# Attention in a two-layer block: the squares of q and their high part move from ScalarE to VectorE

## The reference

```
def rms_norm(x, g):
    xf = x.astype(jnp.float32)
    y = xf * lax.rsqrt(jnp.mean(xf * xf, axis=-1, keepdims=True) + EPS)
    return (y * g.astype(jnp.float32)).astype(x.dtype)

def swa_sink_mixer(h, w_in, q_gain, sinks, w_out, k_band, v_band, bias, mask):
    q, z = jnp.split(h @ w_in, 2, axis=-1)
    q = rms_norm(q.reshape(B, T, B_Q_HEADS, B_HD), q_gain) * (B_HD ** -0.5)
    logits = jnp.einsum("bnqkgd,bnskd->bnkgqs", q, k_band).astype(jnp.float32) + bias
    ...
    p = jnp.exp(logits - m)
    probs = p / (jnp.sum(p, axis=-1, keepdims=True) + jnp.exp(sink - m))
    o = jnp.einsum("bnkgqs,bnskd->bnqkgd", probs.astype(v_band.dtype), v_band)
    o = o.reshape(B, T, B_W) * jax.nn.silu(z)
```

## Time and profile before

| | before |
|---|---|
| median of three runs | 1569.17 us |
| lowest and highest run | 1562.31 and 1571.47 us |
| span of the profiled execution | 1562.4 us |
| VectorE busy | 893.4 us (57%) |
| ScalarE busy | 751.1 us (48%) |
| GpSimd busy | 258.1 us (17%) |
| mean granted TensorE clock | 0.999 |

### The profile page before, as it was taken

The page is one execution under the profiler, slowest core; times in us unless marked ns, Lnnn a source line. Parts: engine busy times, 40 slices in busy tenths (PEclk is TensorE's granted clock), DMA queues, the critical chain, the costliest instruction groups (busy, mean ns, idle before and its releaser), DMA issues.

```text
span 1562.4 us, 20671 instructions
## 1 busy us (share of the span) xinstructions
PE 1531.7 (98%) x7650; PEld 1222.0 (78%) x7650; DVE 893.4 (57%) x1681; ACT 751.1 (48%) x1310; POOL 258.1 (17%) x453
## 2 busy tenths in 40 slices
PE   9989999999999999999998999999999999999998
PEld 7878888888878777777776887666678888888877
DVE  5767677776656456666666435554375243443476
ACT  4454455544553346666667314656555241332343
POOL 1033323443313003343343000000000000000000
PEclk9999999999999999999999999999999999999999
DMA  5311111211114332222222231112222223233221
GB/s 202 109 54 54 55 54 55 67 55 55 47 48 153 99 106 73 84 82 68 81 76 68 81 108 63 54 68 68 67 85 91 94 95 108 84 105 95 94 95 54
DMA packets 40163, 127.22 MB, mean 81 GB/s; under 512 B 4576, under 2 KB 9104, under 8 KB 40064
## 3 DMA queue, kind: packets, MB, share of 16 engines
q1 hardware_dynamic: 38112, 121.65, 24.1%
q0 software_dynamic: 1040, 3.27, 0.6%
q10 hardware_dynamic: 912, 0.99, 0.2%
HBM read 122.69 MB, written 2.15 MB: 80 GB/s over the span
## 4 chain that ended last, share of the span: by engine, by line
PE 90%; DVE 5%; ACT 3%; POOL 1%; issue 1%; DMA 0%; SPq 0%; POOLq 0%; ACTq 0%; DVEq 0%
PE ps L833 87%; PE ps L1196 2%; PE ps L976 1%; DVE wl L1945 1%; ACT L L1751 1%; POOL L L2761 1%; DVE h L2595 1%; DVE mo L2589 1%; POOL uc L2731 0%; POOL masks L2729 0%; DVE L L2452 0%; DVE up L2080 0%; DMA wraw<-in_wa 0%; DVE xm L2582 0%; ACT wh L1340 0%
## 5 line engine op out<-in xcount | busy, mean ns | idle before, releaser
L833 PE MATMUL ps<-xr,wh 128*128 128x512 f32 x2752 | 880.1, 401 | 3.5 <-DVE xr L2388 1.2
L833 PEld LDWEIGHTS ps<-xr,wh 128*128 128x128 f32 x2752 | 505.7, 188 | 129.6 <-issue 30.5
L833 PE MATMUL ps<-xr,wl 128*128 128x512 f32 x1376 | 538.4, 391 | 0.0
L1945 DVE TENSOR_TENSOR wl<-wraw,wh 128x1024 fp32r<-128x1024 f32 x214 | 264.5, 1243 | 130.9 <-ACT wh L1340 128.8
L833 PEld LDWEIGHTS ps<-xr,wl 128*128 128x128 f32 x1376 | 258.6, 188 | 56.1
L1340 ACT ACTIVATE wh<-wraw 128x1024 fp32r<-128x1024 f32 x214 | 222.2, 1049 | 85.8 <-PE ps L833 83.8
L833 PE MATMUL ps<-xm,wh 128*128 128x512 f32 x640 | 198.8, 392 | 5.1 <-DVE xm L2582 2.7
L833 PEld LDWEIGHTS ps<-xm,wh 128*128 128x128 f32 x640 | 119.5, 188 | 33.5 <-DVE xm L2582 4.0
L2761 POOL TENSOR_SCALAR L<-L,m 128x256 f32<-128x256 f32 (+1 forms) x128 | 99.2, 794 | 272.2 <-DVE m L2467 272.2
L833 PE MATMUL ps<-xm,wl 128*128 128x512 f32 x320 | 124.7, 390 | 0.0
L1983 DVE SCALAR_TENSOR_TENSOR qkv<-cin,gains,qkv 128x512 f32<-128x512 f32 x96 | 77.3, 807 | 10.6 <-ACT qkv L1370 9.7
(11 more groups left out here) (265 smaller groups left out, 1749.7 us busy)
## 6 DMA issues: line engine op xcount, KB each, us to landing
wraw<-in_wa SPq DMA_DIRECT2D x48, 512.0 KB, 3.7
wraw<-in_wb SPq DMA_DIRECT2D x32, 512.0 KB, 4.0
wraw<-in_wu SPq DMA_DIRECT2D x32, 512.0 KB, 3.6
wraw<-in_wd SPq DMA_DIRECT2D x32, 512.0 KB, 3.7
wraw<-in_wao SPq DMA_DIRECT2D x16, 512.0 KB, 3.7
wraw<-in_wbo SPq DMA_DIRECT2D x16, 512.0 KB, 3.9
wraw<-in_wc SPq DMA_DIRECT2D x16, 512.0 KB, 3.7
bias<-rel_rows SPq DMA_DIRECT2D x16, 256.0 KB, 3.8
```

Source lines behind the costliest of these rows:

```text
L833: return e.matmul(out, w, x, start=start, stop=stop, skip_group_check=True)
L1945: e.tensor_tensor(m.wl[:, i % N_SPLIT, :], m.raw[:, i % N_RAW, :], m.wh[:, i % N_SPLIT, :].bitcast(F), ALU.subtract).then_inc(s.wlo, 1)
```

## The change

ScalarE's part of `qsquares` is gone. VectorE's part now makes all three: the square in float32, the square again with a rounded output, and the remainder. The waits that ScalarE's part had stand ahead of them on VectorE. The signals are the same, now given by VectorE. The part is called at the same place of `follow`.

```
--- ScalarE's program
     @part
-    def qsquares(j):
-        r = m.flat[j % 2]
-        e.wait_ge(s.q, j + 1)
-        if j == 0:
-            e.wait_ge(s.rows, 16)
-        elif j == 1:
-            for g in range(4):
-                e.wait_ge(s.kpad[g], 32)
-        else:
-            e.wait_ge(s.tr_p, 4 * (j - 2) + 4)
-        e.activation(r[:, 512:1024], m.qb[:, j % 3, :], ACT.Square).then_inc(s.hn_sq, 1)
-        e.wait_ge(s.hn_sq, 2 + j + 1)
-        e.activation(m.LR[:, j % 2, 2, :], r[:, 512:1024], ACT.Copy).then_inc(s.hn_hi, 1)
--- VectorE's program
     @part
     def qsquares(j):
-
+        q, sq = m.qb[:, j % 3, :], m.flat[j % 2][:, 512:1024]
+        e.wait_ge(s.q, j + 1)
+        if j == 0:
+            e.wait_ge(s.rows, 16)
+        elif j == 1:
+            for g in range(4):
+                e.wait_ge(s.kpad[g], 32)
+        else:
+            e.wait_ge(s.tr_p, 4 * (j - 2) + 4)
+        e.tensor_tensor(sq, q, q, ALU.mult).then_inc(s.hn_sq, 1)
+        e.tensor_tensor(m.LR[:, j % 2, 2, :], q, q, ALU.mult).then_inc(s.hn_hi, 1)
+        e.wait_ge(s.hn_sq, 2 + j + 1)
         e.wait_ge(s.hn_hi, j + 2)
         e.tensor_tensor(m.LR[:, j % 2, 3, :], m.flat[j % 2][:, 512:1024], m.LR[:, j % 2, 2, :].bitcast(F),
                         ALU.subtract).then_inc(s.hn_lo, 1)
```

More of the change, by code:

```diff
@@ L1720, in qsquares @@
     @part
-    def qsquares(j):
-        r = m.flat[j % 2]
-        e.wait_ge(s.q, j + 1)
-        if j == 0:
-            e.wait_ge(s.rows, 16)
-        elif j == 1:
-            for g in range(4):
-                e.wait_ge(s.kpad[g], 32)
-        else:
-            e.wait_ge(s.tr_p, 4 * (j - 2) + 4)
-        e.activation(r[:, 512:1024], m.qb[:, j % 3, :], ACT.Square).then_inc(s.hn_sq, 1)
-        e.wait_ge(s.hn_sq, 2 + j + 1)
-        e.activation(m.LR[:, j % 2, 2, :], r[:, 512:1024], ACT.Copy).then_inc(s.hn_hi, 1)
-    @part
     def qnorm(j):
```

## The result

The changed kernel takes 1575.63 us (median of six runs, 1575.46 to 1579.41), the kernel before 1568.62 us beside it. The ratio is 1.006 with a 95% interval from 1.0044 to 1.0075: slower by some 7 us by the medians, 9 us by the ratio. The profiled spans are further apart, 1573.7 against 1562.4 us.

What follows compares the result with a forecast made beforehand. TensorE was taken to bound the kernel, busy 1531.7 of 1562.4 us, with VectorE's and ScalarE's latency counting where it waits. 14 x 0.64 = 9.0 plus 0.4 gave +9.4 us on the median 1569.17: 1578.6 us, range 1568 to 1586.

Steps and rivals of the forecast that it cites:

- The unmarked wait: At the head sum TensorE waits for the remainder (line 2429) each pair, too briefly to be marked: 0.23 us a period.
- The order on VectorE: In VectorE's in-order queue the squares stand behind lines 2465 and 2467, so cannot use the 2.67 us idle before.
- The slip: The remainder starts 1.56 instead of 0.92 us after line 2467's start: 0.64 us a pair, 9.0 us for j=1 to 14.
- The 0.05 charged for GpSimd: Delay of VectorE's added work by GpSimd's multiplication of the probabilities (line 2761): 0.05 us a period.
- The 0.10 behind the double wait: The remainder, waiting for both squares, starts 0.10 us late behind its last releaser.
- The last pair: At j=15 0.37 us of cover is left, but TensorE waits for line 2761, held up by the added work: 0.4 us.
- They delay each other: VectorE's instructions and GpSimd's pieces of line 2761 slow one another; 0.05 us a period charged to VectorE.
- No gain from ScalarE's relief: ScalarE loses 20.0 us and rounds a weight tile 1.25 us earlier in a period, costed at no gain.
- Full blocking: Each multiplication and the remainder's start stand behind a whole GpSimd piece: slip 1.31 us, 18 in all, 1588 us; chance 0.13.
- The not-slower case: Squares run in VectorE's idle 2.67 us between lines 2031 and 2465; TensorE's stalls go: 4 us less, 1565 us; chance 0.07.
- The hidden case: The 0.83 us distance is no wait, or multiplications are quick as a copy: 0 to 4 us, 1569 to 1573; chance 0.20.

Runs made afterwards that it cites:

- experiment 1: Changed kernel with VectorE's three instructions issued directly behind q's tile, ahead of line 2465: 1564.94 us, ratio 0.9982 to the kernel before.
- experiment 2: Changed kernel with a third VectorE multiplication, its result overwritten, between the two squares: 1589.6 us, ratio 1.0136 to the kernel before.
- experiment 5: Kernel of experiment 1 with a third multiplication, also placed early, behind line 2031: 1559.97 us in one run.
- experiment 6: Changed kernel with GpSimd's line of probabilities, pairs 0 to 14, held until the next pair's remainder is done: 1576.73 us in one run.
- experiment 7: Changed kernel without the remainder's wait on the first square: 1576.79 us in a single run.
- experiment 8: Changed kernel with the rounded square made as a copy of the first square, not a second multiplication: 1578.74 us in one run.
- experiment 3: Changed kernel with the float32 square back on ScalarE; VectorE makes rounded square and remainder: 1567.81 us, ratio 1.0007 to the kernel before.
- experiment 9: Kernel of experiment 1 again, with more runs beside the kernel before: 1565.59 us, ratio 0.9975.
- the early kernel: The kernel of experiment 1, measured again in experiment 9: 1564.94 and 1565.59 us.

## Why the prediction was right

The way and the size were right: +9.4 us forecast, +7.0 by the medians and 10 at equal clock, and the range holds the measured time. The mechanism is the forecast one. That the size came so close is in part luck (see "What cancels").

- **The unmarked wait.** It was argued from a constant distance of 0.83 us and three spacings in the earlier trace rows. Shown: moved out of the way (experiment 1) it gave 0.23 us a period, the figure priced; with the path longer by 0.56 us (the change) or 1.26 (experiment 2), the period grew by all of it.
- **The order on VectorE.** Shown by the timeline after and by experiments 1 and 5. It is what made the change a loss: in the program's text the squares follow the laying down of q's tile, but in VectorE's queue line 2465 stands between.
- **The slip.** Forecast 0.64, measured 0.56. Line 2421 took 0.65 and not 0.69, and line 2422 followed 0.57 after its start and not 0.60. The 0.05 charged for GpSimd was not there (experiment 6). The 0.10 behind the double wait was there (0.11 from line 2422's end at 648.32), and experiments 7 and 8, with single waits, show 0.03.
- **The last pair.** Forecast 0.4, measured 1.7. This is the step that failed: "They delay each other", priced at 0.05 for VectorE and at 0.4 for what TensorE waits for GpSimd. VectorE lost nothing, and GpSimd a good deal. In the period shown after the change its first piece took 1.24 us, and its second, from 648.46, 1.96. It got in once in the row of squares, remainder and line 1930, behind line 2422. The gap before the remainder is not what let it in: in experiment 2, where the third multiplication follows without a gap, and in experiment 7 the first piece took 1.23 and 1.24 as well. Behind a single multiplication (experiments 3 and 8) it took 0.71. What decides when it gets in is open. In mid-stage TensorE asks for the pieces 5.6 us after the reciprocal, at the last pair at once.
- **What cancels.** In the stage the change cost 0.7 (j=1) + 7.3 (thirteen slips) + 0.6 (the two odd periods, cause open) + 1.7 (last pair) = 10.3, against 9.0 + 0.4 forecast. The slips were smaller than forecast, the last pair and the odd periods, which the sum did not have, made up for it.
- **No gain from ScalarE's relief.** Shown as far as it goes: ScalarE rounds the weights earlier (line 1340 at +0.09 behind line 1740), and the periods are longer by the slip and no less. No run moved the rounding of the weights by itself.
- **The rivals.** Full blocking of VectorE did not come; only GpSimd stood through whole instructions of the other. The not-slower case was the right mechanism for another kernel: with the squares in the 2.7 us it takes 4.0 us less than the kernel before (experiment 9), as had been worked out. The hidden case is refuted by experiment 2.

What the Trainium skill says in "SBUF — State Buffer", section "Who interferes with whom", that the later of the two blocks fully, fits GpSimd here: its second piece, where the shortest take 0.36, took 1.96 beside the remainder and line 1930. For VectorE the runs show less than a piece: 0.10 us in experiment 2, 0.06 and 0.04 on copy and remainder in experiment 8, each against j=0, and 0 in the changed kernel.

## What to carry to other kernels

When work moves to an engine that has free time, ask where that free time lies in its queue: an in-order engine that idles in front of a wait can only use the idle time with what stands ahead of the wait. A busy row that hides its ends can still hold a wait in each period; a constant distance between a releaser and its waiter, equal to that of a marked wait, finds it, and the spacing of the starts prices it. Where GpSimd's result is needed next, look at what a row of VectorE instructions with two SBUF inputs does to it: here a piece of GpSimd's that takes 0.37 us undisturbed took 1.95 at the last pair, and the change cost 1.7 us there.

## What the runs showed of the hardware

**Half-clock stretches.** TensorE's granted clock falls to half (1.2 instead of 2.4 GHz) for short stretches, which differ from run to run of one kernel: the early kernel's profile has 22 us of them in the first experiment and 6 in the ninth. Windows of the profile show it (the clock is the third column from the end). The kernel before:

```profile
111.00:115.00 4.00, 4.00 (x16) 3.53 (x16) 3.85 (x9) 2.27 (x3) 2.20 (x2) 0.57 0.37 131
```

The changed kernel:

```profile
435.00:437.00 2.00, 1.83 (x8) 1.53 (x9) 1.97 (x6) 1.93 (x3) 0.00 (x0) 0.76 0.03 8
437.00:443.00 6.00, 6.00 (x22) 5.23 (x22) 5.12 (x8) 2.88 (x5) 0.00 (x0) 0.51 0.25 87
```

Before the second, from 430 to 436 us and still at full clock, TensorE was busy for 3.90 of 6 us; in the kernel before it has 4.48 of these 6 us and 7.92 of the 10 from 430 to 440, and stayed at full clock. So the pauses of this part did not bring the fall each time. The stretches make most of the spread of the runs: before's spans are 1560.7 us at a mean clock of 1.000, 1563.7 to 1564.1 at 0.998, and 1569.2 to 1570.2 at 0.993. One run does not fit: 1572.1 us at 0.945. The changed kernel's three runs at 0.998 have 1573.7 to 1573.9, 10 us more than before's at that clock. A median of a few runs moves by several us with it; spans of equal clock, and better the period of a stage, which came out alike to 0.01 us in three kernels (17.86), compare more closely.

**A multiplication of a tile with itself** takes VectorE about 692 ns behind a long instruction, 684 with a rounded output, as the remainder with its two tiles takes 692: it is no quicker. Behind the short reciprocal it takes 652 ns, with a rounded output too (651, experiment 3).
